# Differential heads: the product of probabilities and values in full fp32 from one copy, in place of three fp32r products of high and low parts

## The reference, cut to what matters

```
def step(i):
    ...
    s = jnp.einsum('bqhnd,bkhnd->bhnqk', q_i, k).astype(jnp.float32) * scale
    s = s + bias[None, :, None]
    s = jnp.where(mask, s, -jnp.inf)
    p = jax.nn.softmax(s, axis=-1)
    a = p[:, :, 0] - lam * p[:, :, 1]
    o = jnp.einsum('bhqk,bkhd->bqhd', a.astype(v.dtype), v)
    o = rmsnorm(o, g_sub) * (1.0 - lam_init)
```

## Time and profile before

| | |
|---|---|
| median of 3 runs | 2805.71 us (2801.96 to 2806.47) |
| the profiled execution | 2801.12 us, of which the span is 2799.4 us |
| attention in it | from about 570 to 1376 us |
| PE busy | 2725.3 us (97%) |
| DVE busy | 1756.6 us (63%) |
| ACT busy | 1344.5 us (48%) |
| POOL busy | 629.6 us (22%) |

### The profile page before, as it was taken

How to read it: one execution, slowest core, us unless ns; L and a number is a source line. 1 busy time by engine, 2 the same in 40 slices (tenths; PEclk the granted TensorE clock), 3 DMA queues, 4 the chain that set the end, 5 groups by cost and what they waited for, 6 DMA issues and landing times.

```text
span 2799.4 us, 36795 instructions
## 1 busy us (share of the span) xinstructions
PE 2725.3 (97%) x13362; PEld 2253.3 (80%) x13362; DVE 1756.6 (63%) x2495; ACT 1344.5 (48%) x2413; POOL 629.6 (22%) x558
## 2 busy tenths in 40 slices
PE   8999999989999999999999999999999999999998
PEld 6888888878787787877788788888888888888887
DVE  6211111169889889899846778887777544435567
ACT  5121111168788788788523545464444433322233
POOL 5220021026746646556411100000000000000012
PEclk9999999999999999999999999999999999999999
DMA  5443343464434514414346755565345555546566
GB/s 190 131 153 101 104 136 113 144 148 98 105 83 97 128 52 118 123 41 120 106 128 217 260 204 199 186 237 201 134 149 196 180 186 209 185 159 224 203 219 240
DMA packets 287660, 434.49 MB, mean 155 GB/s; under 512 B 19648, under 2 KB 134592, under 8 KB 287488
## 3 DMA queue, kind: packets, MB, share of 16 engines
q1 hardware_dynamic: 241664, 368.41, 42.4%
q10 hardware_dynamic: 45056, 63.05, 6.2%
q0 software_dynamic: 768, 0.79, 0.1%
HBM read 280.27 MB, written 151.91 MB: 154 GB/s over the span
## 4 chain that ended last, share of the span: by engine, by line
PE 68%; DVE 5%; ACT 4%; issue 3%; POOL 0%; ACTq 0%; POOLq 0%; DVEq 0%
PE ml_ps L2845 7%; PE ml_ps L2843 7%; PE ml_ps L2844 7%; PE ml_ps L2813 7%; PE ml_ps L2815 7%; PE ml_ps L2816 7%; PE at_ps_t L1486 5%; PE at_ps_s L1462 4%; PE at_ps_s L1468 3%; PE mo_acc L1801 2%; PE mo_acc L1803 2%; PE mo_acc L1802 2%; PE at_ps_o L1501 2%; PE at_ps_o L1502 2%; ACT at_probs L1313 2%
## 5 line engine op out<-in xcount | busy, mean ns | idle before, releaser
L1361 DVE TENSOR_REDUCE at_nmax<-at_ps_s 128x1 f32<-128x1024 f32 (+7 forms) x384 | 346.6, 906 | 37.0 <-PE at_ps_s L1468 34.8
L2813 PE MATMUL ml_ps<-ml_h_hiM,ml_w_hi 128*128 128x512 f32 x896 | 349.1, 390 | 1.0 <-DVE ml_t L2635 0.9
L2816 PE MATMUL ml_ps<-ml_h_hiM,ml_w_lo 128*128 128x512 f32 x896 | 348.7, 389 | 0.0
L2815 PE MATMUL ml_ps<-ml_h_loM,ml_w_hi 128*128 128x512 f32 x896 | 348.7, 389 | 0.0
L2845 PE MATMUL ml_ps<-ml_b_hi,ml_a_lo 128*128 128x512 f32 x896 | 348.6, 389 | 0.0
L2844 PE MATMUL ml_ps<-ml_b_lo,ml_a_hi 128*128 128x512 f32 x896 | 348.6, 389 | 0.0
L2843 PE MATMUL ml_ps<-ml_b_hi,ml_a_hi 128*128 128x512 f32 x896 | 348.6, 389 | 0.0
L598 DVE SCALAR_TENSOR_TENSOR pj_out_sb<-pj_acc,pj_out_sb 128x512 fp32r<-128x512 f32 x96 | 66.4, 691 | 424.1 <-ACT pj_out_sb L534 424.1
L1370 DVE TENSOR_TENSOR at_p_lo<-at_ps_t,at_p_hi 128x512 fp32r<-128x512 f32 x480 | 280.0, 604 | 35.8 <-ACT at_p_hi L1331 32.7
L1331 ACT ACTIVATE at_p_hi<-at_ps_t 128x512 fp32r<-128x512 f32 x480 | 248.5, 533 | 87.6 <-PE at_ps_t L1486 48.0
L2490 POOL TENSOR_SCALAR ml_ss<-ml_ss 128x1 f32<-128x1 f32 x16 | 17.6, 1099 | 1183.7 <-ACT ml_junk L2583 1183.4
(11 more groups left out here) (264 smaller groups left out, 5981.3 us busy)
## 6 DMA issues: line engine op xcount, KB each, us to landing
ml_a_raw<-ua SPq DMA_DIRECT2D x112, 512.0 KB, 3.9
qk<-pj_out_sb ACTq DMA_DIRECT2D x64, 512.0 KB, 2.8
ml_w_raw<-in_w_up_dram SPq DMA_DIRECT2D x64, 512.0 KB, 5.1
ua<-ml_t SPq DMA_DIRECT2D x128, 256.0 KB, 2.6
ml_b_raw<-in_w_down_dram SPq DMA_DIRECT2D x56, 512.0 KB, 4.9
at_q<-qk SPq DMA_DIRECT2D x96, 256.0 KB
at_k<-qk SPq DMA_DIRECT2D x96, 256.0 KB
ua<-ml_x SPq DMA_DIRECT2D x96, 256.0 KB, 2.6
```

What stands on the lines that cost most here:

```text
L1361: dve.tensor_reduce(nmax[:, par, sc.a, s, sc.part:sc.part + 1], ps_s[:, sc.g % 2, 0:sc.width], AX.X, ALU.max, negate=True).then_inc(maxed, 1)
L2813: pe.matmul(to, hi, h_hi[m][:, k, :], start=begins and k == 0, stop=False, skip_group_check=not begins)
L2815: pe.matmul(to, hi, h_lo[m][:, k, :], start=False, stop=False, skip_group_check=not begins)
L2816: last = pe.matmul(to, lo, h_hi[m][:, k, :], start=False, stop=k == 3, skip_group_check=not begins)
```

## The change

The values of the differential heads are no longer split. In `project` DVE copies the tile (`tensor_copy`) and ACT has nothing to do for it; only 128 of 256 columns are stored and later loaded. In `attend` a turned slot of a differential block is copied once, unsplit, to `p_whole` (which lies where `p_lo` lies): by ACT for J below 3 and for odd key groups of J = 3, by DVE for the 8 even ones of J = 3. The copy frees the slot. The three fp32r products become one matmul whose operands are both fp32. The semaphores are counted anew to fit. In the table of durations the "lo" step of most differential tiles is gone, and the product costs 0.0018 us per column in place of 0.00135. `RUSH` stays as it was.

```
+def split(job):
+    return job.what == "qk" or (job.what == "val" and job.n == FOX)
...
+def on_scalar(b, t):
+    return b.kind == DIFF and (b.J < 3 or t.j % 2 == 1)
...
+            self.p_whole = r.sb("p_whole", [P, 4, 512])
...
+                    used = 256 if job.n == FOX else P
+                    act.dma_start(vals[job.n, :, job.rb * P:(job.rb + 1) * P, 0:used].rearrange("i p c -> p i c"),
+                                  src.rearrange("p (i c) -> p i c", c=256)[:, :, 0:used]).then_inc(stored[job.out % OR], 16)
...
+                elif not split(job):
+                    dve.wait_ge(multiplied, m + 1)
+                    dve.wait_ge(stored[job.out % OR], 16 * (job.out // OR))
+                    dve.tensor_copy(f32(out_view(job, 0)), acc_view(job)).then_inc(evacuated, 1)
...
-            ring.append(("lo", t))
+            ready = ("hi", t) if on_scalar(b, t) else ("lo", t)
+            ring.append(ready)
...
-            walk.step("hi", t, "ACT", 0.07 + 0.00084 * width, at + RUSH["hi"],
-                      [("turn", t), ("pv", turns[t.n - PRING]) if t.n >= PRING else None], 0.16 + 0.00084 * width)
-            walk.step("lo", t, "DVE", 0.07 + 0.00104 * width, at + RUSH["lo"], [("hi", t)], 0.15 + 0.00104 * width, line="ring")
-            cost = (0.0009 if fox else 0.00135) * width
+            turned = [("turn", t), ("pv", turns[t.n - PRING]) if t.n >= PRING else None]
+            if fox or on_scalar(b, t):
+                walk.step("hi", t, "ACT", 0.07 + 0.00084 * width, at + RUSH["hi"], turned, 0.16 + 0.00084 * width)
+            if not on_scalar(b, t):
+                walk.step("lo", t, "DVE", 0.07 + 0.00104 * width, at + RUSH["lo"], [("hi", t)] if fox else turned,
+                          0.15 + 0.00104 * width, line="ring")
+            cost = (0.0009 if fox else 0.0018) * width
...
+                    to = (p_whole if blocks[t.b].kind == DIFF else p_hi)[:, t.n % PRING, t.off:512]
+                    act.activation(to, ps_t[:, at % TRING, t.off:512], ACT.Copy).then_inc(hi_ready, 1)
...
+                    if blocks[t.b].kind == DIFF:
+                        dve.wait_ge(x_ready, at + 1)
+                        dve.wait_ge(p_used, t.n - PRING + 1)
+                        dve.tensor_copy(p_whole[:, t.n % PRING, t.off:512], ps_t[:, at % TRING, t.off:512])\
+                           .then_inc(x_free, 1)
+                        continue
...
+            def wait_free(at):
+                if at in hi_at:
+                    pe.wait_ge(hi_ready, hi_at[at])
+                else:
+                    pe.wait_ge(x_free, x_no[at])
...
-                        pe.matmul(out, v[:, 0:P], p_hi[:, ring, t.off:512], start=start, stop=False)
-                        pe.matmul(out, v[:, P:2 * P], p_hi[:, ring, t.off:512], start=False, stop=False)
-                        last = pe.matmul(out, v[:, 0:P], p_lo[:, ring, t.off:512], start=False, stop=t.end)
+                        last = pe.matmul(out, f32(v[:, 0:P]), p_whole[:, ring, t.off:512], start=start, stop=t.end)
```

More of the change, by code:

```diff
@@ L126, in __init__ @@
             self.k2 = r.sb("k2", [P, 6, 2, 512], F32R)
+        with ExitStack() as shared:
+            r = Room(nc, shared, "atw")
+            r.sb("p_hi_place", [P, 4, 512])
+            self.p_whole = r.sb("p_whole", [P, 4, 512])
         with ExitStack() as third:
@@ L221, in project @@
         splits_after[m].append(z)
-    hi_no = {m: sum(1 for job in jobs[:m + 1] if job.what in ("qk", "val")) for m in range(len(jobs))}
+    hi_no = {m: sum(1 for job in jobs[:m + 1] if split(job)) for m in range(len(jobs))}
     carry_job = next(m for m, job in enumerate(jobs) if job.what == "carry")
@@ L506, in store @@
                 else:
-                    act.dma_start(vals[job.n, :, job.rb * P:(job.rb + 1) * P, :].rearrange("i p c -> p i c"),
-                                  src.rearrange("p (i c) -> p i c", c=256)).then_inc(stored[job.out % OR], 16)
+                    used = 256 if job.n == FOX else P
+                    act.dma_start(vals[job.n, :, job.rb * P:(job.rb + 1) * P, 0:used].rearrange("i p c -> p i c"),
+                                  src.rearrange("p (i c) -> p i c", c=256)[:, :, 0:used]).then_inc(stored[job.out % OR], 16)
             for t in range(3):
@@ L529, in _ @@
                 if job.out is not None:
-                    if job.what != "logit":
+                    if split(job):
                         act.wait_ge(multiplied, m + 1)
@@ L1048, in attend @@
             ring += 1
+    hi_no, hi_at, x_no, his, frees = {}, {}, {}, 0, 0
+    for (what, arg), at in ring_at.items():
+        if what == "turn" and (blocks[arg.b].kind == FOX or on_scalar(blocks[arg.b], arg)):
+            his += 1
+            hi_no[arg.n] = his
+        if what == "turn" and on_scalar(blocks[arg.b], arg):
+            hi_at[at] = his
+        else:
+            frees += 1
+            x_no[at] = frees
     last_turn = {t.b: t for t in turns}
@@ L1082, in attend @@
         k1, k2, q1, q2, p_hi, p_lo = keep.k1, keep.k2, keep.q1, keep.q2, keep.p_hi, keep.p_lo
+        p_whole = keep.p_whole
         k_loaded, q_loaded = keep.k_loaded, keep.q_loaded
@@ L1130, in attend @@
         last_turned = max(turns, key=lambda t: ring_at["turn", t])
+        last_copy = max(n for n, (what, arg) in enumerate(steps) if what in ("hi", "lo") and arg is last_turned)
         last_spread = max(pairs, key=lambda pair: ring_at["spread", pair[0].qb])[0].qb
@@ L1277, in gpsimd @@
                         if d >= 4:
-                            pool.wait_ge(x_free, ring_at["var", diffs[d - 4]] + 1)
+                            pool.wait_ge(x_free, x_no[ring_at["var", diffs[d - 4]]])
                         pool.tensor_tensor(squares[:, d % 4, :], sums, sums, ALU.mult).then_inc(squared, 1)
@@ L1281, in gpsimd @@
                     q = arg.qb
-                    pool.wait_ge(x_free, ring_at["var", arg] + 1)
+                    pool.wait_ge(x_free, x_no[ring_at["var", arg]])
                     if q >= 2:
@@ L1288, in scalar @@
             first_hi = next(arg for what, arg in steps if what == "hi")
-            for what, arg in steps:
+            for n, (what, arg) in enumerate(steps):
+                if n == last_copy + 1:
+                    then()
                 if what == "corr":
@@ L1495, in tensor @@
                         pe.wait_ge(o_free, b.n)
-                    pe.wait_ge(x_free, ring_at["turn", t] + 1)
+                    wait_free(ring_at["turn", t])
                     out = ps_o[:, t.off:512]
@@ L1531, in tensor @@
                     last.then_inc(x_ready, 1)
-        return Attention(sync, gpsimd, scalar, vector, tensor, len(scores), ring_at["turn", last_turned] + 1, ring, scored,
+        return Attention(sync, gpsimd, scalar, vector, tensor, len(scores), ring_at["turn", last_turned] + 1, frees, scored,
                          exped, x_ready, x_free, p_used, o_free)
```

23 lines of the change are left out of this document (9 added, 14 removed).

## The result

The changed kernel takes 2819.87 us in the median of four runs (2817.91 to 2824.21), the kernel before 2805.85 us (2801.96 to 2806.47). The ratio is 1.0057, with an interval from 1.0043 to 1.0071: slower by 14 us, or by 16 us if one goes by the ratio. The forecast was 2817 us. The profiled execution of the changed kernel is its slowest, 2824.21 us, with a span of 2822.3 us, and the profiled one of before (2801.12 us) is among its fastest. The two profiles are therefore 23 us apart where the medians are 14.

The account below looks back on a forecast made before the run. The prediction took PE to bound the changed differential stretches: +26 us for the product, −14 of waits and −0.6 in the projection gave +11.4 on 2805.7, rounded to 2817 us. The range was 2797 to 2836 us.

Parts of the forecast that it names:

- the product: Differential heads' product of probabilities and values on PE: a fourth pass, 31.6 us of work, 26 us on the path.
- relief: Differential heads: PE's waits for subtraction, exponentials and mixing shrink 3.5 us per head, 14 us; projection's last ACT copy, 0.6 us.
- the order: Planner's new sequence of scores and products on PE in the attention: put at zero, 5 us to both sides.
- I take the upper bound: Full fp32 product on PE taken as four passes, 0.93 us per tile, where three fp32r passes take 0.70 us.
- The share on the path: Differential stretch: 19.7 of 23.7 us of products per head lie on the chain of waits, 83%, applied to the fourth pass.
- another wait may take the place: Differential heads: lower bound of 0 for waits won back, as ACT still copies and the fourth pass delays the ring.
- the first rival: DVE bounds the attention and its relief wins; forgetting stretches would shrink 3 us or more; 2787 us, chance 0.12.
- Two passes: Differential product's two instructions pass the columns only once each, 31.6 us less on PE: −40 us, 2765 us, chance 0.04.
- DVE is the true bound: Attention: DVE's relief wins back more than 32 us of PE's idle time, faster; up to −19 us, 2787 us; chance 0.12.
- Nothing is won back: Differential heads: waits for subtraction become waits for ACT, whole fourth pass counts: +31 us, 2836 us, chance 0.15.
- The two sides cancel: Differential stretches: 20 to 32 us of PE's idle time won back, so no difference, 2806 us, chance 0.17.

Follow-up runs that it names:

- before_order: Kernel before with only the planner's differential product duration changed from 0.00135 to 0.0018 us per column, same instructions in another order: 2817.67 us, +13.0.
- after_135: Changed kernel planned with the old product duration, 0.00135 us per column, same instructions in another order: 2823.57 us, +19.0 against the kernel before.
- copy_3r: Changed kernel with three fp32r products of the single copy in place of the fp32 one, low parts left out: 2809.85 us, +5.2 against the kernel before.
- copy_3r_135: Changed kernel with three fp32r products of the copy, low parts left out, planned with the old duration 0.00135: 2799.49 us, −5.1 against the kernel before.
- copy_4r: Changed kernel with four fp32r products of the single copy in place of the fp32 one, low parts left out: 2830.45 us, +25.8 against the kernel before.
- after_urgent: Changed kernel with product duration 0.00168 us per column and the planner's urgencies set anew, same instructions: 2801.94 us, −2.6 against the kernel before.
- copy_3r_urgent: Changed kernel with three fp32r products of the copy, low parts left out, duration 0.00139, urgencies set anew: 2796.75 us, −6.8 against the kernel before.
- before_4: Kernel before with a fourth fp32r product, low by low, per differential tile, order kept: 2830.06 us, +25.4.
- after_act: Changed kernel with all copies of differential tiles to p_whole on ACT, none on DVE: 2817.23 us, +13.7 against the kernel before.
- before_var: Kernel before with the product with the mean in fp32r with two columns instead of fp32, squares rounded: 2796.52 us, −7.0.

## Why the prediction was right, and where it was not

The direction is right, and the measured +14 us is close to the sum of +11.4. The terms are not right, and that their errors cancel is luck. The sum had 26 us for the product, 14.6 us of relief (0.6 of them in the projection) and nothing for the order. Two routes lead from the kernel before to the changed one, and they give the terms different sizes:

| term | forecast | with the new number, 0.0018 | with the old number, 0.00135 |
|---|---|---|---|
| the number in the plan | 0 | +13.0 (before_order) | about −4 (after_135 to the changed kernel) |
| relief of DVE | −14.6 | −7.8 (before_order to copy_3r) | −5.1 (copy_3r_135) |
| the fp32 product | +26 | about +10 (copy_3r to the changed kernel) | +24.1 (copy_3r_135 to after_135) |

In the row of the relief the order is not quite kept, since the subtractions are gone from the plan. Each column adds up to about the measured loss because of how it is made, so that it does so proves nothing. What the table shows is that the terms are no constants: what the product or the number costs depends on the order in which it is measured. The relief is 7 to 10 us short on the two routes. The product and the order are each near the forecast on one route and far off on the other.

**The product.** The direction holds: one fp32 product costs more than three fp32r passes. The price was off. The step is the term "I take the upper bound", four passes or 0.93 us per tile. It measured 0.86 us, so over 136 full tiles PE gains 0.16 x 136 = 22 us in place of 31.6. The Trainium skill gives true fp32 four passes (page "FP8 and Floating Point Precision", section "TensorE Precision Notes"); the trace agrees within a tenth, 0.86 us being 3.7 times 0.23. copy_4r against the changed kernel measures that difference, 10.6 us (11.8 by the differences to before). Next to copy_3r the product costs about 10 us (9 by the differences to before, 11 by the ratios), next to copy_3r_135 24.1 us, where 26 were in the sum. At equal clock the two prices are nearer, 12 us and 18 to 19: at 0.995 the changed kernel took 2821.34 us (one execution) and copy_3r 2808.48 to 2809.95 (four). With both orders set anew it costs 4 us (after_urgent at −2.6, copy_3r_urgent at −6.8, each beside its own before); that comparison is between two groups and two orders and is no better than a few microseconds.

**The share on the path.** 83% was taken from the chain of waits. For a true pass in the order of before it holds, 80% in before_4. It doesn't carry over to another order: of the same 31.6 us copy_4r shows 65% over copy_3r, and of the 22 us of the fp32 product about 10 us are seen with the new number and, at equal clock, 18 to 19 with the old one.

**The relief.** This step failed on every route: 14 us were forecast, 3.5 per head, from waits of PE that would go. The waits for the subtraction did go from the differential heads, but PE's idle time in the attention fell only from 47.3 to 44.2 us. With the new number the wait for the copy on DVE took their place, with the old one a longer wait for exponentials (19.8 us in copy_3r_135, 14.4 in the kernel before). The prediction had that another wait may take the place as its lower bound, and named ACT; in the changed kernel it came on DVE, and moving the copies to ACT turned it into the wait for exponentials (after_act). What the relief is worth when the order fits is shown by copy_3r_urgent, 6.8 us, 0.6 of them forecast for the projection: about half of what was forecast.

**The order.** The other step that failed is "Either sign is possible, I put it at zero with 5 us to both sides". Both signs did come: +13.0 us from the number alone in the kernel before, about +10 us in the three-product version (copy_3r_135 to copy_3r), about −4 us in the changed kernel. But the width was far too small. The same instructions of the changed kernel took 2801.94, 2807.3, 2819.87 and 2823.57 us in four orders, 22 us from first to last, against the 10 us that the prediction allowed. In these runs an order does well when the plan's number is near the true price: 0.00135 with three passes, 0.0018 rather than 0.00135 with the fp32 product. Setting the urgencies anew takes the loss away (after_urgent).

How the order costs time is only partly settled. In before_order 2.8 of 15 us of the attention are idle time of PE and 12.2 are longer busy time of the same instructions. The stretches at half clock explain 8.5 us of these at most, and the one at the attention's start, 10.2 us in place of 6.8, another 1.7. But the two profiles make the clock's part look large, since before was profiled at a mean granted clock of 0.998 and its other executions go down to 0.995. At the same 0.995 before took 2805.92 to 2808.73 us in that group (six executions) and before_order 2816.01 us (one): 7 to 10 us of its loss are left with the clock equal. The clock is given to three digits; half a unit of the last is 2.8 us at half clock, worth 1.4 us at most. Likewise at 0.996 the changed kernel took 2817.91 and 2818.40 us and after_urgent 2802.16 to 2802.87 us (four). There the loss of some 15 us is about what PE idles more in the attention, 13.5 us. What makes up the 7 to 10 us of before_order wasn't tried; PE's idle time has only 2.8 us between the two profiles.

The relief, too, is larger at equal clock: at 0.995 copy_3r_urgent took 2794.95 to 2797.06 us and before beside it 2806.07 to 2806.69, 10 us in place of 6.8.

**The single claims.** 320 matmuls at L1552, 224 of them 512 wide: right. Starts 0.46 us apart: 0.43. The differential stretch to grow by 3 us: as the heads were cut here it grew by 5, from 70 to 75, and by 11 where the clock fell. DVE to lose some 75 us of work: 61 by the page, whose busy time counts overlapping records once; by the groups the subtractions went from 280.0 to 185.7 us and 21.0 us of copies came, 73 less. DVE near 64 us in 895 to 990 us: 61.5 in this window of the changed kernel,

```profile
895.00:990.00 95.00, 88.29 (x435) 63.16 (x434) 61.50 (x131) 64.87 (x150) 58.34 (x39) 0.95 0.39 99
```

L1552 at a quarter of the chain: 28.2%. The forgetting stretches unchanged: 129 to 130 us became 127, which is about the bound of 3 us that the prediction set for the first rival; a small part of it may be at work. The first score 0.6 us earlier: its weights come at 568.75 us against 569.50 in the earlier trace rows, 0.75 earlier, with ACT's copy gone from the chain:

```profile
566.93 0.69 DVE L609 COPY pj_out_sb<-pj_acc 128x512 f32<-128x512 f32 x1 [4.75 <-PE pj_acc L727]
...
568.78 0.47 PE L1510 MATMUL at_ps_s<-at_k,at_q 128*128 128x512 f32 x1 [1.89 <-PEq L251]
```

**The rivals.** Two passes are out, by 0.43 us per instruction. "DVE is the true bound" needed more than 32 us won back; the best order with three passes wins 6.8. "Nothing is won back" held nearly as it stands for PE's idle time in the changed kernel, which fell by 3 us. With four real passes (copy_4r) the time is 2830 us, not far from this rival's 2836; the cheaper product kept the changed kernel from it. "The two sides cancel" is what the same instructions do in a better order (after_urgent, −2.6 us).

## What to carry to other kernels

Where a planner or a hand-made order is fitted to durations, a change of one duration moves everything, and the order can matter more than the arithmetic: the same instructions differ by 22 us here, and the same dearer product costs 24 us in one order and 10 in another (18 to 19 and 12 at equal clock). So run both the old and the new work in both orders before you put a price on the edit, and fit the order anew before you reject it. An engine that is relieved of work gives time back only if what is left on it comes at the right moment; here one 0.68 us copy behind a 1.22 us maximum made PE wait 2.2 us per head. A long wait is no proof of a cost, though: with these copies on ACT the wait went and the time fell by 1 us only. And count small products too: sixteen times eight fp32 instructions of one column were worth 7 us, as much as the whole relief of DVE. Last, compare the granted clock of two executions before you read one profile against the other.

## What was new about the hardware

- A product of two fp32 operands with 512 columns is two instructions of 0.43 us, 0.86 us in all, and so cheaper than four fp32r passes, 0.93 us. copy_4r shows it as a whole, 10 to 12 us over 136 full tiles.
- An fp32 product of one column is two instructions too, 1.02 us for four products; in fp32r with two columns four products take 0.58 us, and the kernel wins 7.0 us, all of the 16 x 0.44 us of PE: none of it was hidden.
- PE's granted clock falls to one half within the attention, in stretches of 3.4 or 6.8 us. In the changed kernel each begins 0.1 to 2.6 us behind the end of a wait of 0.9 to 2.3 us. The reverse doesn't hold: before waits 2.22 us ahead of 620.70 us and more than ten times 1.0 to 1.2 us behind it, and its profile has no such stretch behind the attention's start; nor has that of before_var. Which waits bring the clock down no run here shows. In the timeline of the changed kernel four transposes take 0.63 us at 932.71 and 1.05 us at 935.11, inside such a stretch. Executions of one kernel differ by it: after_urgent took 2797.54 us at a mean granted clock of 0.998 and 2804.99 at 0.995, before 2800.66 at 0.998 and 2805.92 to 2808.73 at 0.995.
